# Token sums in half passes, four tiles first in the last round, and a shorter end for the last tile

## The chip, the cores and the metric

The kernel runs on one core of a Trainium2 chip. The metric is the device time of one execution in microseconds (us), lower being better; the time before is the median of 3 runs. TensorE (PE) does the matmuls, and its weight loads are counted apart (PEld). VectorE (DVE), ScalarE (ACT) and GpSimd (POOL) do elementwise work, and SyncE (SP) issues DMAs. The engines run side by side, each through its own list of instructions in order, and wait for each other on semaphores.

## The reference

One layer of a hybrid attention and state-space network over 128 context and 512 latent tokens, 640 in all, with 1024 channels, in float32. The change touches its last part, the MLP and the last layer norm:

```python
h  = layer_norm(x) * (1 + sc2) + sh2
ff = jnp.square(jax.nn.relu(h @ p['w_mlp1'] + p['b_mlp1'])) @ p['w_mlp2'] + p['b_mlp2']
x  = layer_norm(ALPHA * x + g2 * ff, p['ln2_g'], p['ln2_b'])
```

## The kernel before

Each float32 operand of a matmul is kept as two parts, an upper and a lower one, and each product takes three matmuls. ScalarE writes the upper part of a weight block (split_hi, tile whi), VectorE subtracts it from the block to get the lower one (split_lo, wlo, L2280), and TensorE waits for that on the semaphore lo_done.

The 4096 hidden channels come in four rounds of 1024. In each, a first product makes hidden channels for all 640 tokens, and a second one adds them into five tiles of 128 tokens (tile 0 is the context, 1 to 4 are latent), each in two halves of 512 channels (c = 0, 1).

- Round 0 makes its hidden channels in 8 units of 48 matmuls (the first four in two halves of 24). For each, VectorE adds the bias and takes the maximum with 0 (L2927), which also frees the unit's PSUM banks, squares (L2929) and subtracts the upper part (L2932); ScalarE makes that upper part between them. TensorE begins unit n when VectorE's L2927 of unit n - 2 is done. The second product goes over (c, b), where b is a half of the 1024 hidden channels: 12 matmuls for each tile, so 60 for each (c, b), and VectorE adds each finished bank into xo (L2987).
- Rounds 1 to 3 use Strassen's scheme for the first product: 7 products in place of 8 for each 2 by 2 block. It needs four sums of the token operand, each with an upper and a lower part. They are made once, in round 0, by operand_sum on VectorE (L2956, ten sums, and L2965, four lower parts) and upper_sum on ScalarE (L2211). Before the change eight sums and two lower parts stand between round 0's units, two sums and two lower parts behind them, ahead of the second product's first addition. TensorE needs them at the start of round 1. GpSimd makes the sums of the weights for each block (L934 to L940) and two lower parts (L943).
- The last round's second product (last_products) has its own order, the table LAST. For c = 0 it does three tiles with b = 0, then the same three with b = 1; for that it needs the second lower part (L2280). Then come single units of 24 matmuls, whose c = 1 weights are split into the tiles hh and hl (w3h, w3l; last_lo, L3064, two of them, after the first and the second unit on VectorE). For each unit VectorE runs last_unit: add the bank to xo (L3055), multiply by the gate row g2r (L3057), add ALPHA times x1 (L3058), and statistics (L3060). When a tile is whole it gathers the statistics (L2307), adds EPS (L3085), and ScalarE takes the root. One unit later, in finish, it inverts the root (L3068) and makes two weighing passes over 1024 channels (L2321: less the mean, times ln2_g; L2322: times the inverse, plus ln2_b), and SyncE stores the tile (L792). The last tile's second half comes in two units of 256 channels.

The gate rows g2r and x1 of tiles 0 to 2 are loaded in the last round (L780, L778), when the memory that they take is no longer needed by Strassen's scheme. The whole order is written out by hand.

## Time and profile before

| What | us |
|---|---|
| median of 3 runs | 1574.17 (1572.31 to 1575.41) |
| the profiled execution | 1572.93 |
| its span, first to last instruction | 1571.2 |
| TensorE busy | 1505.6 (96%) |
| VectorE busy | 1015.6 (65%) |
| ScalarE busy | 688.3 (44%) |
| GpSimd busy | 208.0 (13%) |

An engine's busy time is the sum over its instructions, and the share is of the span. Matmuls overlap in a pipeline, so TensorE at 96% says that it seldom stands idle. Times in the rows below count from the span's start. Round 0's first product runs from about 1128 to 1186, the last round's second product from 1501 to the end.

### The profile page before, as it was taken

To read this page: it belongs to the slowest core of one execution; us is meant where nothing else is said; L and a number is where in the kernel's file an instruction comes from. 1 tells how busy PE (TensorE), PEld (TensorE's weight loads), DVE (VectorE), ACT (ScalarE), POOL (GpSimd) and SP (SyncE) were. 2 spreads that over 40 slices of the span, in tenths; PEclk is the share of its full clock that TensorE was granted. 3 is DMA by queue.
4 is the path that set the end of the run, shared out by engine and by line. 5 is a ranking of instruction groups with operands and counts; after the bars stand their busy time and mean duration, and the time that the engine had idled before them with its cause. 6 is when DMAs were issued, how large, how long until landed. Compare 5 with 4: busy or idle time off the path is not lost.

```text
span 1571.2 us, 25180 instructions
## 1 busy us (share of the span) xinstructions
PE 1505.6 (96%) x10114; PEld 1397.2 (89%) x10114; DVE 1015.6 (65%) x1410; ACT 688.3 (44%) x1258; POOL 208.0 (13%) x227
## 2 busy tenths in 40 slices
PE   4999999999999989999999999999989999999997
PEld 2899999999999989898766899999988898998976
DVE  5666566658555688988876443438876462653768
ACT  2443333343563266777676342323523262451630
POOL 1011122100101100000000001000001441611700
PEclk9999999999999999999999999999999999999999
DMA  9555555543777767877620346235212132131251
GB/s 318 177 177 193 176 185 178 179 137 118 227 231 260 246 232 243 266 225 220 226 105 27 126 154 201 95 107 189 94 54 81 54 108 81 54 108 54 81 174 67
DMA packets 152511, 244.62 MB, mean 156 GB/s; under 512 B 8112, under 2 KB 110240, under 8 KB 149344
## 3 DMA queue, kind: packets, MB, share of 16 engines
q1 hardware_dynamic: 129232, 174.59, 33.4%
q0 software_dynamic: 12304, 47.72, 8.3%
q10 hardware_dynamic: 10880, 20.97, 5.2%
q8 instruction: 68, 1.11, 0.3%
q14 instruction: 27, 0.22, 0.0%
HBM read 196.63 MB, written 46.63 MB: 155 GB/s over the span
## 4 chain that ended last, share of the span: by engine, by line
PE 78%; DVE 12%; ACT 6%; issue 1%; DMA 1%; SPq 1%; ACTq 0%; DVEq 0%
PE acc L957 57%; PE tp L957 18%; DVE wlo L2280 2%; ACT arena L1914 2%; PE tp L1424 1%; ACT whi L1692 1%; DVE arena L2554 1%; PE tp L1085 1%; DMA arena<-in_w_mod 1%; DVE arena L2385 1%; DMA arena<-decay_sums_t 1%; DVE arena L2555 1%; ACT whi L2072 1%; DVE wlo L2755 1%; DVE arena L2956 1%
## 5 line engine op out<-in xcount | busy, mean ns | idle before, releaser
L957 PE MATMUL acc<-hh,whi 128*128 128x322 f32 (+1 forms) x1068 | 288.2, 319 | 8.0 <-DVE cst L2927 3.6
L957 PE MATMUL acc<-hl,whi 128*128 128x322 f32 (+1 forms) x1068 | 281.7, 313 | 0.0
L957 PE MATMUL acc<-hh,wlo 128*128 128x322 f32 (+1 forms) x1068 | 281.0, 312 | 0.0
L957 PEld LDWEIGHTS acc<-hh,whi 128*128 128x128 f32 x1068 | 189.2, 191 | 12.7 <-issue 10.4
L957 PEld LDWEIGHTS acc<-hl,whi 128*128 128x128 f32 x1068 | 190.7, 191 | 0.0
L957 PEld LDWEIGHTS acc<-hh,wlo 128*128 128x128 f32 x1068 | 190.4, 191 | 0.0
L957 PE MATMUL acc<-whi,hh 128*128 128x256 f32 x640 | 183.1, 286 | 0.0
L957 PE MATMUL acc<-whi,hl 128*128 128x256 f32 x640 | 179.7, 281 | 0.0
L957 PE MATMUL acc<-wlo,hh 128*128 128x256 f32 x640 | 179.7, 281 | 0.0
L2280 DVE TENSOR_TENSOR wlo<-raw,whi 128x2048 fp32r<-128x2048 f32 x62 | 143.5, 2315 | 34.9 <-ACT whi L1692 34.9
L1692 ACT ACTIVATE whi<-raw 128x2048 fp32r<-128x2048 f32 x62 | 118.2, 1907 | 76.9 <-PE tp L957 53.9
L957 PE MATMUL tp<-arena 128*32 128x256 f32 (+4 forms) x774 | 135.0, 373 | 10.0 <-DVE arena L2573 3.7
L2385 DVE SCALAR_TENSOR_TENSOR arena<-arena,colp 128x642 f32<-128x642 f32 x128 | 113.6, 888 | 16.9 <-DVE arena L2383 1.2
L957 PEld LDWEIGHTS acc<-whi,hh 128*128 128x128 f32 x640 | 120.6, 188 | 0.6 <-issue 0.2
L957 PEld LDWEIGHTS acc<-wlo,hh 128*128 128x128 f32 x640 | 120.5, 188 | 0.2
L957 PEld LDWEIGHTS acc<-whi,hl 128*128 128x128 f32 x640 | 120.5, 188 | 0.0
L957 PEld LDWEIGHTS tp<-arena 128*128 128x128 f32 (+1 forms) x774 | 85.0, 164 | 35.0 <-issue 19.3
L1914 ACT ACTIVATE arena<-arena,time_steps 128x128 f32<-128x128 f32 x320 | 97.7, 391 | 25.6 <-PE acc L957 18.0
L1704 ACT ACTIVATE arena<-acc 128x644 f32<-128x644 f32 (+2 forms) x94 | 47.8, 508 | 126.2 <-PE acc L957 126.1
L1762 ACT ACTIVATE arena<-arena 128x642 f32<-128x642 f32 x32 | 23.8, 743 | 112.4 <-DVE arena L2385 112.4
L957 PE MATMUL acc<-whi,fh 128*128 128x512 f32 x176 | 69.7, 396 | 1.6 <-DVE wlo L2280 1.6
L957 PE MATMUL acc<-wlo,fh 128*128 128x512 f32 x176 | 69.6, 395 | 0.0
(361 smaller groups left out, 3127.5 us busy)
## 6 DMA issues: line engine op xcount, KB each, us to landing
raw<-in_w_in SPq DMA_DIRECT2D x38, 1024.0 KB, 8.6
raw<-in_w_mlp SPq DMA_DIRECT2D x32, 1024.0 KB, 5.3
arena<-in_w_mod SPq DMA_DIRECT2D x24, 1024.0 KB, 8.2
arena<-decay_sums_t ACTq DMA_DIRECT2D x40, 512.0 KB, 6.0
arena<-xs_nat SPq DMA_DIRECT2D x8, 1024.0 KB, 10.7
raw<-in_w_ssd_o SPq DMA_DIRECT2D x8, 1024.0 KB, 6.6
y_nat<-arena POOLq DMA_DIRECT2D x6, 1024.0 KB, 7.6
arena<-y_nat SPq DMA_DIRECT2D x6, 1024.0 KB, 6.0
```

Of the source, the lines that this page charges most:

```text
L957: return pe.matmul(out, l, r, start=first, stop=last)
L1085: last = pe.transpose(dst, cvs[:, n % 2, tok(t):tok(t) + P], ident)
L1424: last = pe.transpose(tp[:, j // 4, (j % 4) * P:(j % 4 + 1) * P], pr[:, u, j * P:(j + 1) * P], ident)
L1692: act.activation(whi[:, slot], raw[:, slot], ACT.Copy).then_inc(hi["sem"], step(hi))
L1704: act.activation(dst, src, func).then_inc(free["sem"], step(free))
L1762: act.activation(cvs[:, n % 2], cvo[:, n % 2], ACT.Silu).then_inc(silu["sem"], step(silu))
L1914: last = act.activation(ee[:, b, d, r], abc[:, b, d, r], ACT.Relu, bias=dta[:, c, h:h + 1], scale=-1.0)
L2072: last = act.activation(whi[:, slot, k], raw[:, slot, k], ACT.Copy, scale=colp[:, n:n + 1])
L2280: dve.tensor_tensor(wlo[:, slot], raw[:, slot], whi[:, slot].bitcast(F32), ALU.subtract).then_inc(lo["sem"], step(lo))
L2385: ins = dve.scalar_tensor_tensor(o, x[:, t:t + NCONV], w(t), o, ALU.mult, ALU.add)
L2554: do(dve.tensor_tensor(ee[:, b], ee[:, b], cbm[:, :, g].unsqueeze(2).broadcast_to([P, 2, R, P]), ALU.mult))
L2555: dve.tensor_tensor(ee[:, b, 0], ee[:, b, 0], ee[:, b, 1], ALU.add).then_inc(m_ok["sem"], step(m_ok))
```

## The change

1. Round 0: no operand sum and no lower part stands between the units any more. Eight sums stand now ahead of the second product's first addition on VectorE, the other two and the four lower parts between its halves c = 0 and c = 1. The upper parts on ScalarE move with them.
2. Last round: four tiles, not three, are done with b = 0 and then b = 1, ahead of the units with c = 1. The lower parts of the c = 1 weights (last_lo) stay behind the first and the second unit.
3. The first weighing pass (begun) stands right behind the statistics, ahead of the wait for the root; finish keeps the inverse and the second pass.
4. For the last tile, GpSimd multiplies xo by the gate row and adds ALPHA times x1 beforehand, with three new instructions of 1024 channels. VectorE's unit for that tile has then two elementwise instructions in place of three: the bank times the gate row, and the sum.
5. The last tile's second weighing pass and its store come in two halves of 512 channels.

```diff

-    LAST = [(t, c, 0, 2 * BW) for t, c in ((0, 0), (1, 0), (2, 0), (0, 1), (1, 1), (2, 1), (3, 0), (3, 1), (4, 0))]
+    LAST = [(t, c, 0, 2 * BW) for t, c in ((0, 0), (1, 0), (2, 0), (3, 0), (0, 1), (1, 1), (2, 1), (3, 1), (4, 0))]
     LAST += [(4, 1, 0, BW), (4, 1, BW, BW)]
...
         sp.dma_start(lnr2[:, 1], a["ln2_b"][0].partition_broadcast(P)).then_inc(s["rows2_in"], 16)
-        for t in range(NT):
+        for t in range(NT - 1):
             sp.wait_ge(s["final_ok"], t + 1)
             dst = y_p[0] if t == 0 else y_s[0, (t - 1) * P:t * P]
             sp.dma_start(dst, xo[:, t]).then_inc(s["out_done"], 16)
-        sp.wait_ge(s["out_done"], 16 * NT)
+        for b in range(2):
+            sp.wait_ge(s["final_ok"], NT + b)
+            cols = slice(b * 2 * BW, (b + 1) * 2 * BW)
+            sp.dma_start(y_s[0, (NT - 2) * P:, cols], xo[:, NT - 1, cols]).then_inc(s["out_done"], 16)
+        sp.wait_ge(s["out_done"], 16 * (NT + 1))

...
                 step(raws[b], 2)
+
+        t = NT - 1
+        po.wait_ge(s["rows2_in"], 16 * 4)
+        po.wait_ge(s["acc_free"], U_MLP + KT + 3 * 2 * NT)
+        po.tensor_tensor(xo[:, t], xo[:, t], g2r[:, 1], ALU.mult).then_inc(sums["sem"], step(sums))
+        po.tensor_scalar(x1[:, t], x1[:, t], ALPHA, None, ALU.mult).then_inc(sums["sem"], step(sums))
+        po.wait_ge(sums["sem"], value(sums))
+        po.tensor_tensor(xo[:, t], xo[:, t], x1[:, t], ALU.add).then_inc(sums["sem"], step(sums))

...
                 pe.wait_ge(lo["sem"], due(lo))
-                for i in range(3):
+                for i in range(NT - 1):
                     if b == 0:
                         step(free)
                         bank_free(i, False)
                     last = ff_products(last_bank(i), i, *whole[0][b], b, waits=i == 0)
                     if b:
                         last.then_inc(ready["sem"], step(ready))
-            for i in range(3, len(LAST)):
+            for i in range(NT - 1, len(LAST)):
                 t, c, at, n = LAST[i]
...
                 for b in range(2):
-                    if i == 3:
+                    if i == NT - 1:
                         pe.wait_ge(lo["sem"], due(lo))
...
                 step(ready)
-                if n in (3, 4):
-                    upper_sum(n - 3)
                 if n % 2 == 1:
...
             if r == 0:
-                upper_sum(2)
-                upper_sum(3)
+                for n in range(3):
+                    upper_sum(n)
             act.wait_ge(half["sem"], due(half))
             split_hi(0)
             step(ready, NT)
             act.wait_ge(ready["sem"], value(ready))
             split_hi(1)
+            if r == 0:
+                upper_sum(3)
             act.wait_ge(half["sem"], due(half))
...
                     split_lo(n // 2 % 2)
-                if 1 <= n <= 4:
-                    operand_sum(2 * n - 2)
-                    operand_sum(2 * n - 1)
-                elif n in (5, 6):
-                    operand_sum(10 + n - 5)

...
             if r == 0:
-                for n in (8, 9, 12, 13):
+                for n in range(8):
                     operand_sum(n)
...
                     split_lo(1)
+                    if r == 0:
+                        for n in range(8, 14):
+                            operand_sum(n)
                 else:
...
             dve.wait_ge(ready["sem"], due(ready))
-            dve.tensor_tensor(xo[:, t, cols], xo[:, t, cols], last_bank(i)[:, 0:n], ALU.add).then_inc(free["sem"], step(free))
-            dve.wait_ge(free["sem"], value(free))
-            do(dve.tensor_tensor(xo[:, t, cols], xo[:, t, cols], g2r[:, min(t, 1), cols], ALU.mult))
-            do(dve.scalar_tensor_tensor(xo[:, t, cols], x1[:, t, cols], ALPHA, xo[:, t, cols], ALU.mult, ALU.add))
+            if t < NT - 1:
+                dve.tensor_tensor(xo[:, t, cols], xo[:, t, cols], last_bank(i)[:, 0:n], ALU.add).then_inc(free["sem"], step(free))
+                dve.wait_ge(free["sem"], value(free))
+                do(dve.tensor_tensor(xo[:, t, cols], xo[:, t, cols], g2r[:, min(t, 1), cols], ALU.mult))
+                do(dve.scalar_tensor_tensor(xo[:, t, cols], x1[:, t, cols], ALPHA, xo[:, t, cols], ALU.mult, ALU.add))
+            else:
+                if c == 0:
+                    dve.wait_ge(s["sum_ok"], LANDED + 4 * 3 * S_BLOCKS + 3)
+                dve.tensor_tensor(x1[:, t, cols], last_bank(i)[:, 0:n], g2r[:, 1, cols], ALU.mult).then_inc(free["sem"], step(free))
+                dve.wait_ge(free["sem"], value(free))
+                do(dve.tensor_tensor(xo[:, t, cols], xo[:, t, cols], x1[:, t, cols], ALU.add))
             for b in range(at // BW, (at + n) // BW):
...

+        def begun(t):
+
+            if t == 0:
+                dve.wait_ge(s["rows2_in"], 16 * 6)
+            do(dve.scalar_tensor_tensor(xo[:, t], xo[:, t], mv[:, t, 0:1], lnr2[:, 0], ALU.subtract, ALU.mult))
+
         def finish(t):
             dve.wait_ge(dev["sem"], due(dev))
             do(dve.reciprocal(mv[:, t, 2:3], mv[:, t, 2:3]))
-            weighed(t, xo[:, t], lnr2).then_inc(s["final_ok"], 1)
+            for b in range(2 if t == NT - 1 else 1):
+                cols = slice(b * 2 * BW, (b + 1) * 2 * BW) if t == NT - 1 else slice(0, D)
+                dve.scalar_tensor_tensor(xo[:, t, cols], xo[:, t, cols], mv[:, t, 2:3], lnr2[:, 1, cols],
+                                         ALU.mult, ALU.add).then_inc(s["final_ok"], 1)

...
             if whole is not None:
-                if whole == 0:
-                    dve.wait_ge(s["rows2_in"], 16 * 6)
                 finish(whole)
                 whole = None
+            if i in (0, 1):
+                last_lo(i)
             if i in WHOLE:
                 whole = WHOLE[i]
                 dve.wait_ge(dv["sem"], value(dv))
                 gathered(whole)
                 dve.tensor_scalar(mv[:, whole, 2:3], mv[:, whole, 1:2], EPS, None, ALU.add).then_inc(var["sem"], step(var))
-            if i in (0, 1):
-                last_lo(i)
+                begun(whole)
         finish(whole)
```

What VectorE finds in round 0 behind the first block's split_lo (hl and hh are the operand's parts, cst the unit's channels), before:

```order
L2280 TENSOR_TENSOR wlo<-raw,whi 128x2048 [waits hi_done]
L2956 TENSOR_TENSOR arena<-hh 128x1280 [waits x_in3_then_x1_out]
L2956 TENSOR_TENSOR arena<-hl 128x1280 [waits dve_step]
L2927 TENSOR_SCALAR cst<-tp,colp 128x640 [waits acc_ready,dve_step]
L2929 TENSOR_TENSOR time_steps<-cst 128x640 [waits acc_free]
L2932 TENSOR_TENSOR fl<-time_steps,fh 128x640 [waits square_ok,relu_ok]
L2956 TENSOR_TENSOR arena<-arena 128x1280
L2956 TENSOR_TENSOR arena<-hh 128x1280 [waits mod_in7_then_t_sum]
```

and after:

```order
L2292 TENSOR_TENSOR wlo<-raw,whi 128x2048 [waits hi_done]
L2939 TENSOR_SCALAR cst<-tp,colp 128x640 [waits acc_ready]
L2941 TENSOR_TENSOR time_steps<-cst 128x640 [waits acc_free]
L2944 TENSOR_TENSOR fl<-time_steps,fh 128x640 [waits square_ok,relu_ok]
L2939 TENSOR_SCALAR cst<-tp,colp 128x640 [waits acc_ready]
```

The two sums between the split and the next unit's L2927 (L2939 now) are gone, and so are those behind that unit.

VectorE at the end of round 0's first product, from the last split_lo on, before:

```order
L2280 TENSOR_TENSOR wlo<-raw,whi 128x2048 [waits hi_done]
L2956 TENSOR_TENSOR hl_full<-hh,arena 128x4x320
L2956 TENSOR_TENSOR hl_full<-hl_full,hl 128x4x320 [waits dve_step]
L2965 TENSOR_TENSOR t_lo<-arena,t_hi 128x1280 [waits x_in_then_t_hi,mod_in7_then_t_sum]
L2965 TENSOR_TENSOR hl<-hl_full,hh 128x4x320 [waits x_in_then_t_hi]
L2987 TENSOR_TENSOR arena<-arena,acc 128x512 [waits acc_ready]
L2280 TENSOR_TENSOR wlo<-raw,whi 128x2048 [waits hi_done]
```

and after:

```order
L2292 TENSOR_TENSOR wlo<-raw,whi 128x2048 [waits hi_done]
L2963 TENSOR_TENSOR arena<-hh 128x1280 [waits x_in3_then_x1_out]
L2963 TENSOR_TENSOR arena<-hl 128x1280 [waits dve_step]
L2963 TENSOR_TENSOR arena<-arena 128x1280 [waits dve_step]
L2963 TENSOR_TENSOR arena<-hh 128x1280 [waits mod_in7_then_t_sum]
L2963 TENSOR_TENSOR arena<-hl 128x1280 [waits dve_step]
L2963 TENSOR_TENSOR arena<-arena 128x1280 [waits dve_step]
L2963 TENSOR_TENSOR arena<-hh,arena 128x1280 [waits mod_in7_then_t_sum]
L2963 TENSOR_TENSOR arena<-arena,hl 128x1280 [waits dve_step]
L2994 TENSOR_TENSOR arena<-arena,acc 128x512 [waits acc_ready,mod_in7_then_t_sum]
L2292 TENSOR_TENSOR wlo<-raw,whi 128x2048 [waits hi_done]
```

Eight sums, each waiting for the one before it, now stand ahead of the first addition of a bank and of the next split_lo.

GpSimd at the end of its list, after (before, the list ended with the second of these rows):

```order
L947 TENSOR_TENSOR wlo<-time_steps,whi 128x512 [waits mod_in1_then_entry_hi]
L947 TENSOR_TENSOR wlo<-time_steps,whi 128x512 [waits mod_in1_then_entry_hi,mod_in6_then_pool_lo]
L956 TENSOR_TENSOR arena<-arena 128x1024 [waits acc_free,rows2_in,mod_in6_then_pool_lo]
L957 TENSOR_SCALAR arena<-arena 128x1024
L959 TENSOR_TENSOR arena<-arena 128x1024 [waits mod_in0_then_sum_ok]
```

The three last rows are new. The first of them waits for the gate rows (rows2_in), and the second follows it without a wait.

VectorE's end, from the last tile's two units of 256 channels on, before:

```order
L3055 TENSOR_TENSOR arena<-arena,acc 128x256 [waits acc_ready]
L3057 TENSOR_TENSOR arena<-arena 128x256 [waits acc_free]
L3058 SCALAR_TENSOR_TENSOR arena<-arena 128x256 [waits dve_step]
L3060 BN_STATS st<-arena 128x6 [waits dve_step]
L3055 TENSOR_TENSOR arena<-arena,acc 128x256 [waits acc_ready]
L3057 TENSOR_TENSOR arena<-arena 128x256 [waits acc_free]
L3058 SCALAR_TENSOR_TENSOR arena<-arena 128x256 [waits dve_step]
L3060 BN_STATS st<-arena 128x6 [waits dve_step]
L2307 BN_AGGR mv<-st 128x2 [waits dve_step]
L3085 TENSOR_SCALAR mv<-mv 128x1 [waits dve_step]
L3068 RECIPROCAL mv<-mv 128x1 [waits dev_ok]
L2321 SCALAR_TENSOR_TENSOR arena<-arena,mv,raw 128x1024 [waits dve_step]
L2322 SCALAR_TENSOR_TENSOR arena<-arena,mv,raw 128x1024 [waits dve_step]
```

and after:

```order
L3073 TENSOR_TENSOR arena<-acc,arena 128x256 [waits acc_ready]
L3075 TENSOR_TENSOR arena<-arena 128x256 [waits acc_free]
L3077 BN_STATS st<-arena 128x6 [waits dve_step]
L3073 TENSOR_TENSOR arena<-acc,arena 128x256 [waits acc_ready]
L3075 TENSOR_TENSOR arena<-arena 128x256 [waits acc_free]
L3077 BN_STATS st<-arena 128x6 [waits dve_step]
L2319 BN_AGGR mv<-st 128x2 [waits dve_step]
L3111 TENSOR_SCALAR mv<-mv 128x1 [waits dve_step]
L3087 SCALAR_TENSOR_TENSOR arena<-arena,mv,raw 128x1024
L3091 RECIPROCAL mv<-mv 128x1 [waits dev_ok,dve_step]
L3094 SCALAR_TENSOR_TENSOR arena<-arena,mv,raw 128x512 [waits dve_step]
L3094 SCALAR_TENSOR_TENSOR arena<-arena,mv,raw 128x512
```

Each unit has one instruction less, the first weighing pass stands ahead of the inverse, and the second one is in halves.

## Rows read from the trace of the kernel before

**Rows 1.** TensorE's timeline: start, us, engine, line, operation, tiles, form, [idle, releaser].

```profile
1154.12 0.67 PE L957 MATMUL acc<-hh,whi 128*128 128x320 f32 x2 [3.65 <-DVE cst L2927]
...
1171.29 0.53 PE L957 MATMUL tp<-hh,whi 128*128 128x320 f32 x2 [1.35 <-DVE cst L2927]
```

**Rows 2.** VectorE's timeline around the first of these waits.

```profile
1143.48 0.88 DVE L2927 TENSOR_SCALAR cst<-acc,colp 128x640 f32<-128x640 f32 x1
...
1146.10 0.82 DVE L2932 TENSOR_TENSOR fl<-time_steps,fh 128x640 fp32r<-128x640 f32 x1 [0.88 <-ACT fh L2197]
1147.83 2.29 DVE L2280 TENSOR_TENSOR wlo<-raw,whi 128x2048 fp32r<-128x2048 f32 x1 [0.91 <-ACT whi L1692]
1150.04 1.48 DVE L2956 TENSOR_TENSOR arena<-hh 128x1280 f32<-128x1280 f32 x1
...
1153.09 0.89 DVE L2927 TENSOR_SCALAR cst<-tp,colp 128x640 f32<-128x640 f32 x1
```

**Rows 3.** Stretches: length; PE, PEld, DVE, ACT, POOL busy; PEclk, DMA share, GB/s.

```profile
1114.88:1117.48 2.60, 0.01 (x1) 0.04 (x1) 2.40 (x2) 2.05 (x3) 0.00 (x0) 0.87 0.00 0
1117.48:1120.00 2.52, 2.52 (x9) 2.52 (x10) 2.45 (x6) 1.24 (x1) 0.00 (x0) 0.50 0.42 110
...
1156.00:1158.00 2.00, 2.00 (x10) 2.00 (x9) 1.97 (x3) 0.00 (x0) 0.00 (x0) 0.56 0.01 4
...
1524.55:1528.00 3.45, 3.45 (x15) 2.82 (x16) 3.02 (x6) 0.00 (x0) 0.00 (x0) 1.00 0.00 0
```

**Rows 4.** The chain of waits in order of time: start us, us, engine, tile, line, instructions.

```profile
1171.29 14.29 PE tp L957 x96
...
1196.75 2.80 PE tp L957 x12
```

**Rows 5.** TensorE's timeline, 1508 to 1572, the rows with idle time.

```profile
1511.16 0.50 PE L957 MATMUL acc<-whi,fh 128*128 128x512 f32 x1 [1.64 <-DVE wlo L2280]
...
1524.55 0.51 PE L957 MATMUL acc<-hh,fh 128*128 128x512 f32 x1 [1.91 <-DVE hl L3064]
```

**Rows 6.** VectorE's timeline, 1500 to 1572.

```profile
1507.00 0.82 DVE L3015 TENSOR_TENSOR fl<-cst,fh 128x640 fp32r<-128x640 f32 x1 [2.27 <-ACT cst L2182]
1508.81 2.29 DVE L2280 TENSOR_TENSOR wlo<-raw,whi 128x2048 fp32r<-128x2048 f32 x1 [0.98 <-ACT whi L1692]
1514.34 0.69 DVE L3055 TENSOR_TENSOR arena<-arena,acc 128x512 f32<-128x512 f32 x1 [3.24 <-PE acc L957]
...
1515.79 0.69 DVE L3058 SCALAR_TENSOR_TENSOR arena<-arena 128x512 f32<-128x512 f32 x1
...
1561.98 0.42 DVE L3058 SCALAR_TENSOR_TENSOR arena<-arena 128x256 f32<-128x256 f32 x1
...
1566.84 1.28 DVE L2322 SCALAR_TENSOR_TENSOR arena<-arena,mv,raw 128x1024 f32<-128x1024 f32 x1
```

**Rows 7.** Waits from 1500 to 1572: engine, line, for whom: us, times, longest us.

```profile
DVE arena L3055 <- PE acc L957: 5.1, 3, 3.2
...
DVE arena L3055 <- PE tp L957: 2.2, 1, 2.2
...
DVE mv L3068 <- ACT mv L1699: 0.3, 1, 0.3
```

**Rows 8.** VectorE's timeline in the second round, 1254 to 1258.

```profile
1254.83 1.18 DVE L3015 TENSOR_TENSOR fl<-cst,fh 128x640 fp32r<-128x640 f32 x1 [0.96 <-ACT cst L2182]
...
1256.40 1.33 DVE L2973 TENSOR_TENSOR wlo<-raw,whi 128x512 fp32r<-128x512 f32 x1
```

**Rows 9.** GpSimd's timeline, 1254 to 1258.

```profile
1254.04 1.29 POOL L934 TENSOR_TENSOR time_steps<-raw 128x512 f32<-128x512 f32 x1 [0.72 <-DVE wlo L2973]
1255.41 1.76 POOL L936 TENSOR_TENSOR raw<-raw 128x512 f32<-128x512 f32 x1
```

**Rows 10.** Line 780, the loads of the gate rows: issue to landing.

```profile
DMA to landing us min/median/max: 9.6/10.3/11.1
```

**Rows 11.** Line 792, the stores of the results: issue to landing.

```profile
DMA to landing us min/median/max: 2.6/2.6/2.6
```

## The prediction

> **What bounds the kernel now.** I read the page first. TensorE is busy for 96% of the span and VectorE for 65%: the time is set by TensorE's matmuls, and VectorE counts where TensorE waits for it and behind TensorE's last matmul. So I took TensorE's timeline in the two stretches that the change touches, then VectorE's beside it, then the waits. All times count in the frame of before; what a stretch gains comes off everything behind it.
>
> In round 0 TensorE stands for 3.65 us ahead of unit 4 and for 1.35 us ahead of unit 6, both times for VectorE's L2927 [rows 1]. VectorE's rows show why: the split that unit 4 needs ends at 1150.1, then come two operand sums of 1.5 each, and only at 1153.09 the L2927 of unit 2, which frees what unit 4 waits for [rows 2]. The wait has a price behind it: TensorE's granted clock is 0.56 on average from 1156 to 1158, so the half level (1.2 GHz) for most of it [rows 3].
>
> In the last round TensorE waits twice: 1.64 us for the lower part of the b = 1 weights (L2280), and 1.91 us for last_lo [rows 5]. But VectorE is the nearer limit there. From the first addition at 1514.34 to its end at 1568.12 (1566.84 + 1.28) are 53.78 us [rows 6]. In them it waits 1.9 (5.1 less the 3.24 ahead of the first) and 2.2 for banks and 0.3 for the last root, 4.3 with rounding [rows 6, 7]. So 49.5 us of the stretch are VectorE's own chain.
>
> **Round 0, sums moved away.** Behind the split, L2927 of unit 2 can start at 1150.04 in place of 1153.09 [rows 2]. TensorE went on at 1154.12, 1.03 after that instruction's start [rows 1, 2]; now it goes on at 1151.07, idle 0.6 after 1150.47. Gain 3.05. Units 4 and 5 took from 1154.12 to 1169.94 (1171.29 less 1.35 [rows 1]), 15.8, where the two units 6 and 7 took 14.29 at full clock [rows 4]. I take it that no fall of the clock follows an idle time of 0.6: behind the 1.91 us in the last round it stayed at 1.00, behind 2.60 us at 1114.88 it was 0.50 [rows 3, 5]. Gain 1.5. The 1.35 ahead of unit 6 goes as well, because VectorE has for each pair of units of 14.1 us only two times 3.4 (1143.48 to 1146.92 [rows 2]), a wait of 0.9 and a split of 2.2, some 10 us. With overlaps counted (a matmul's end and the next one's start differ by 0.16) round 0's second product begins 6.1 us earlier, at T = 1179.3.
>
> What is late next? The sums now meet the second product. VectorE's last split of round 0's first product ends at T + 6.7: L2927 to L2932 of unit 7 3.4, ScalarE's upper part in 1.9 of which 1.1 shows, split 2.2. Eight sums of 1.51 (start to start [rows 2]) end at T + 18.8, where before the first bank came at T + 16.8 (14 + 2.8 for a tile [rows 4]): its addition is 2 us late. Behind it stands the split for c = 1, b = 0; ScalarE's upper part for it now waits behind upper_sum(2), which needs sum 8, and so it ends at T + 22.0 and the split at T + 24.3. TensorE asks for it at T + 28: 3.7 us of cover. The other six, 9 us, stand behind the last split of that product at T + 32.3 and end by T + 42, or T + 46 where GpSimd's sums of the weights come between; round 1's first Strassen product asks for them at T + 56. I cost this at nothing. SyncE's load of the next weights waits for the split at T + 24.3 and so is issued 4.7 later than before relative to T; its data are wanted by ScalarE at T + 42, so that is covered too.
>
> **Last round, four tiles first.** The fourth tile with b = 0 gives TensorE 2.8 us of work where it stood 1.64 [rows 4, 5]. Taken alone this removes that wait and, since VectorE gets both last_lo done in time, the 1.91 too; but VectorE's chain starts at the first tile's b = 1. Before, that began at 1511.16 and VectorE's addition 3.18 later at 1514.34 [rows 5, 6]. Now b = 1 begins at 1512.15 at the earliest (1511.16 - 1.64 + 2.80, less the overlap of 0.16), 1.0 later.
>
> **GpSimd's three instructions, a new cost ahead of that point.** Their start is set by the gate rows: issued at 1495.0, landed 11.1 later [rows 10], so 1506.1. No row shows a GpSimd instruction of 1024 elements; those of 512 take 1.29 undisturbed [rows 9], so I take 2.6 (for tensor_scalar between 1.3 and 2.6, chosen 2.6). What they do to VectorE is in the rows: at 1254.83 L3015, with two inputs in SBUF, starts inside GpSimd's L934, which ends at 1255.33, and takes 1.18 instead of 0.82 [rows 6, 8, 9]; L936 then takes 1.76 instead of 1.29, and the split behind it, started at 1256.40, takes 1.33 instead of some 0.7 (instructions of 512 elements take 0.69 [rows 6]), its end 0.56 after L936's [rows 8, 9]. So one of the two stands until the other is through, and they take turns. Here: the first instruction runs from 1506.2 to 1508.8; L3015, due at 1507.00, stands until then and ends at 1509.5; the second one gets its turn from 1509.4 to 1512.0; the split L2280, due at 1509.5, stands until 1512.0 and ends at 1514.2 in place of 1511.1 [rows 6]. TensorE's b = 1 begins at 1514.25, 3.1 later than before, and VectorE's chain at 1517.4. The bounds of this term: 1.0 later (no turn lost) and 5.7 (the second GpSimd instruction, which has no wait of its own, takes its turn ahead of L3015, and the third one ahead of the split).
>
> On the instruction's length the Trainium skill has a price of its own: "GPSIMD Engine Reference", section "Elementwise — side-by-side cycle accounting", gives 4497 ns for a tensor_tensor of 2048 float32, so an estimate of 2.25 us for 1024, where the rows of 512 give 2.6. By the page the chain would start some 0.3 to 0.7 us earlier. The rows decide.
>
> **VectorE's chain and the end.** The last tile loses L3058 three times: once with 512 channels, 0.73 from start to start, twice with 256, 0.46 each [rows 6]: 1.65. The wait for the root (0.3 [rows 7]) goes, since the first weighing pass of 1.3 stands in it, and it was not counted in the 49.5. The second pass in halves costs 0.1 more. Does VectorE still wait for banks? TensorE supplies a c = 1 tile in 5.6, VectorE needs 2.84 for the unit, 0.4 for statistics, 2.7 for both passes, 5.9: it falls behind at once and stays behind, since two units and two splits of 2.2 have already put it 2 us back. So the chain is 49.5 - 1.65 + 0.1 = 48.0 without waits, from 1517.4 to 1565.4. Before it ended at 1568.12: 2.7 earlier. Behind it stands the store: 2.6 from issue to landing for 512 KB [rows 11]. The first half is on its way 0.7 before the second; for the second, half the bytes, I take 0.3 less (between 0, all of it fixed, and 1.3, all of it bytes). Together 3.0.
>
> The Trainium skill, "DMA: Bandwidth & Descriptors", section "Anatomy of one DMA — SWDGE (gpsimd) path", has a fixed 2.0 us and then bytes by 436 GB/s: an estimate of 0.6 less for 256 KB. No run here shows a store of that size at the end; by it the sum would be 0.3 larger.
>
> **Sum.** 6.1 + 3.0 = 9.1. From the profiled execution, 1572.93 (its span 1571.2 and 1.7 around it), this gives 1563.8. That execution lies 1.2 below the median of the runs; against the median, 1574.17 - 9.1 = 1565.0 us, which is what I forecast.
>
> **Rivals.**
> - GpSimd costs VectorE nothing that TensorE sees (its second instruction is short, or VectorE slips in ahead of it). For it: many VectorE instructions in the Strassen rounds lie beside GpSimd's without loss, those that read a bank. Against: L3015 and the split read only SBUF, as in [rows 8]. Then the chain starts at 1515.3, 2.1 earlier: 1563.0.
> - GpSimd keeps its turn over two instructions, because nothing waits between them. Then the split ends at 1516.8, 2.6 later, TensorE has stood 4.5 us, more than the 2.60 behind which the clock fell [rows 3], and loses some 1.7 more at half clock: 1569.3. Against it: in the rows each one waiting got the next turn; but there GpSimd had a semaphore between.
> - The gain in round 0 is smaller: another wait stands where L2927's was (the weights' lower part ends at 1150.1, only 0.4 before TensorE is ready), or the clock falls all the same. That takes 1.5 to 6.1 off: 1566.5 to 1571.1.
> - Slower than before: the eight sums at the head of the second product. If each took more than some 2.0 longer than its 1.5, the split for c = 1, b = 0 would come 16 us late, 12.3 beyond its cover of 3.7, and TensorE would stand that long: over 1577.3 in place of 1565.0. It decides from 3.5 us for a sum. Against it: GpSimd, the only one seen to lengthen such instructions, has nothing to do until the next weights land at about T + 30.
>
> **Chances.** The forecast's case 0.50 (1563.5 to 1566.5), GpSimd free of cost 0.20, GpSimd's double turn 0.10, smaller gain in round 0 0.15, slower 0.05. The range of 1561.8 to 1569.3 holds the first two with the bounds of the store (0 to 1.3) and most of the third and the fourth. A measurement of this kernel can tell about 0.2%, 3.1 us, from no change. All of the first three cases and most of the fourth are faster by more: 0.93. Within it 0.03, slower 0.04.
>
> **What the profile after would show.** Right: TensorE idle ahead of unit 4 for 0.6, nothing ahead of unit 6, granted clock 1.00 from 1151 to 1179; the eight sums from about 1186 to 1198 and no wait of TensorE in the second product; GpSimd's three instructions from about 1500 (1506 less 6.1), L3015 and the split beside them lengthened to some 2.5 and 4.7, a wait of TensorE of 2 us behind four tiles; then VectorE without waits for banks up to its end. Wrong: a split of 2.3 there (first rival), a half clock behind it (second), any TensorE wait between the sums and round 1 (fourth). The forecast fails most easily in the order in which GpSimd and VectorE take turns in those 8 us.

## The result and the profile after

| | before | after |
|---|---|---|
| median of 4 runs each, same chip | 1573.47 (1572.31 to 1575.41) | 1561.68 (1560.47 to 1561.81) |
| ratio, with its 95% interval | | 0.9922 [0.9905, 0.9939] |
| the profiled execution | 1572.93 | 1561.81 |
| its span | 1571.16 | 1560.02 |

The kernel became 11.8 us faster, where 9.1 were forecast. The time lies 0.1 below the forecast's range. The page of after has nearly the same balance as before: busy time by engine, and the chain that ended last by engine. It doesn't say where the time went; only the stretches do.

```profile
PE 1502.3 (96%) x10114; PEld 1393.8 (89%) x10114; DVE 1020.9 (65%) x1408; ACT 688.6 (44%) x1258; POOL 222.0 (14%) x230
...
PE 77%; DVE 13%; ACT 5%; DMA 2%; issue 1%; SPq 1%; ACTq 0%; DVEq 0%
```

**Round 0.** TensorE's timeline of after has one row with idle time from 1119 to 1240, where before had two [rows 1]:

```profile
1150.82 0.53 PE L969 MATMUL acc<-hh,whi 128*128 128x320 f32 x2 [0.62 <-DVE cst L2939]
```

VectorE's rows say why: L2939 (L2927 before) stands now directly behind the split, where two sums stood [rows 2], and the eight sums fill the head of the second product:

```profile
1147.58 2.29 DVE L2292 TENSOR_TENSOR wlo<-raw,whi 128x2048 fp32r<-128x2048 f32 x1 [0.91 <-ACT whi L1704]
1149.79 0.88 DVE L2939 TENSOR_SCALAR cst<-tp,colp 128x640 f32<-128x640 f32 x1
...
1185.76 1.48 DVE L2963 TENSOR_TENSOR arena<-hh 128x1280 f32<-128x1280 f32 x1
...
1196.44 1.49 DVE L2963 TENSOR_TENSOR arena<-arena,hl 128x1280 f32<-128x1280 f32 x1
1197.96 0.69 DVE L2994 TENSOR_TENSOR arena<-arena,acc 128x512 f32<-128x512 f32 x1
1201.07 2.29 DVE L2292 TENSOR_TENSOR wlo<-raw,whi 128x2048 fp32r<-128x2048 f32 x1 [2.42 <-ACT whi L1704]
```

The next table is by stretch: length, busy time of PE, PEld, DVE, ACT and POOL, granted clock, DMA share, GB/s. The second row is the one that answers to the half clock of before from 1156 [rows 3]: the clock holds. The first shows the half clock that both kernels have behind an earlier idle time of 2.6 us, at round 0's start.

```profile
1118.46:1122.00 3.54, 3.54 (x14) 3.54 (x15) 3.40 (x9) 1.36 (x2) 0.00 (x0) 0.55 0.67 181
1150.82:1157.00 6.18, 6.18 (x42) 6.18 (x43) 3.98 (x5) 2.82 (x3) 0.00 (x0) 1.00 0.49 174
```

**The last round.** TensorE's two waits of 1.64 and 1.91 [rows 5] are gone (0.19 is left, at 1520). Its first matmul with b = 1 follows the last one with b = 0 after 0.39, where the others follow each other after 0.23, and it starts 0.05 behind the end of VectorE's split (1505.83, below). So the four tiles cover that split almost to its end, with nothing to spare:

```profile
1505.49 0.40 PE L969 MATMUL acc<-whi,fl 128*128 128x512 f32 x1
1505.88 0.50 PE L969 MATMUL acc<-whi,fh 128*128 128x512 f32 x1
```

VectorE's timeline, from the last operand to the first tile's chain, and then its end, to be held against [rows 6]:

```profile
1500.58 0.82 DVE L3025 TENSOR_TENSOR fl<-cst,fh 128x640 fp32r<-128x640 f32 x1 [2.26 <-ACT cst L2194]
1502.39 3.44 DVE L2292 TENSOR_TENSOR wlo<-raw,whi 128x2048 fp32r<-128x2048 f32 x1 [0.98 <-ACT whi L1704]
1509.08 0.69 DVE L3066 TENSOR_TENSOR arena<-arena,acc 128x512 f32<-128x512 f32 x1 [3.25 <-PE acc L969]
1509.80 1.69 DVE L3068 TENSOR_TENSOR arena<-arena 128x512 f32<-128x512 f32 x1
...
1555.94 0.16 DVE L3091 RECIPROCAL mv<-mv 128x1 f32<-128x1 f32 x1
1556.14 1.41 DVE L3094 SCALAR_TENSOR_TENSOR arena<-arena,mv,raw 128x512 f32<-128x512 f32 x2
```

GpSimd's three new instructions beside it:

```profile
1500.61 3.07 POOL L956 TENSOR_TENSOR arena<-arena 128x1024 f32<-128x1024 f32 x1 [20.08 <-issue]
1503.66 4.81 POOL L957 TENSOR_SCALAR arena<-arena 128x1024 f32<-128x1024 f32 x1
1508.55 2.39 POOL L959 TENSOR_TENSOR arena<-arena 128x1024 f32<-128x1024 f32 x1
```

And the stores of the two halves, where before one of 512 KB took 2.6 [rows 11]:

```profile
DMA to landing us min/median/max: 2.0/2.1/2.1
```

The 11.15 us of the span by stretch, each boundary read in both timelines:

| stretch | before | after | gain | forecast |
|---|---|---|---|---|
| start to TensorE's stop ahead of unit 4 | 1150.47 | 1150.20 | 0.27 | 0 |
| from there to round 0's second product | 34.95 | 28.79 | 6.16 | 6.1 |
| from there to the last round's second product | 315.54 | 315.54 | 0 | 0 |
| from there to VectorE's first addition | 13.38 | 14.55 | -1.17 | -3.1 |
| from there to VectorE's end | 53.78 | 48.47 | 5.31 | 5.8 |
| from there to the span's end | 3.04 | 2.47 | 0.57 | 0.3 |

So the large term was right to 0.1, and the one that failed is the fourth: TensorE waited 0.2 at most for the split behind the four tiles, where 2.1 were forecast. What is left between 11.15 and 11.8 is that before's profiled execution lay 0.5 below its median, and after's 0.1 above.

### The profile page after: what moved, and what is told of

The parts are those of the page before. It is cut to its first block, busy times and chain, and to the rows that moved or that the text cites. A ratio compares the mean times of both kernels' runs of the same rounds, so it can differ in the third digit from the quotient of the medians.

```text
span 1560.0 us, 25183 instructions
## 1 busy us (share of the span) xinstructions
PE 1502.3 (96%) x10114; PEld 1393.8 (89%) x10114; DVE 1020.9 (65%) x1408; ACT 688.6 (44%) x1258; POOL 222.0 (14%) x230
## 4 chain that ended last, share of the span: by engine, by line
PE 77%; DVE 13%; ACT 5%; DMA 2%; issue 1%; SPq 1%; ACTq 0%; DVEq 0%
PE acc L969 57%; PE tp L969 17%; ACT arena L1926 2%; DMA arena<-decay_sums_t 1%; PE tp L1436 1%; DVE wlo L2292 1%; DVE arena L2566 1%; PE tp L1097 1%; DMA arena<-in_w_mod 1%; DVE arena L2397 1%; DVE arena L2567 1%; ACT whi L2084 1%; DVE wlo L2767 1%; PE tp L1483 1%; DVE arena L2600 1%
## 5 line engine op out<-in xcount | busy, mean ns | idle before, releaser
L969 PE MATMUL tp<-arena 128*32 128x256 f32 (+4 forms) x774 | 135.2, 373 | 10.9 <-DVE arena L2585 3.8
L969 PE MATMUL acc<-whi,fh 128*128 128x512 f32 x184 | 72.9, 396 | 0.0
```

Source lines behind the costliest of these rows:

```text
L969: return pe.matmul(out, l, r, start=first, stop=last)
```

## The experiments

Two places were in dispute: which part of round 0's gain is wait and which is clock, and what GpSimd's instructions do to VectorE. Every run has a profile, and the stretches of the table above are read in each; the median is given where there were five runs (four for end_only), beside the ratio to before. Medians move by about 1 us with the chip and the execution, stretches hardly at all: with the sums moved as in after, the one from TensorE's stop to T takes 28.77 to 28.79 in every profile, and the one from T to the last round 315.54 or 315.55 in all but all_head's. So single profiles are compared by their stretches. T is the begin of round 0's second product.

**Does the gain fall into two parts that add up?** sums_only has the move of the sums and nothing else, end_only everything but that.

```diff
 # sums_only: the last round, GpSimd's part, the passes and the store as before
-        LAST = [... (0, 0), (1, 0), (2, 0), (3, 0), (0, 1), (1, 1), (2, 1), (3, 1), (4, 0) ...]
+        LAST = [... (0, 0), (1, 0), (2, 0), (0, 1), (1, 1), (2, 1), (3, 0), (3, 1), (4, 0) ...]
 # end_only: the sums as before
+                    if 1 <= n <= 4:
+                        operand_sum(2 * n - 2)
+                        operand_sum(2 * n - 1)
```

> Before, with only the token sums moved (eight at the head of round 0's second product, the rest between its halves); the last round is as before. Theory A (each part's gain is its own): 6.2 us off the profiled span of 1571.2, so about 1565.0, TensorE idle 0.6 ahead of unit 4 and not at all ahead of unit 6, no half clock from 1150 on. Rival B (part of this gain is given back later, for instance the last round starts earlier but its loads do not): under 5 us off.

> After, with the token sums put back where they were before; all changes of the last round stay. Theory A: 5.0 us off the span of before (11.2 less 6.2), about 1566.2, with the waits of 3.65 and 1.35 us and the half clock back. Rival B (the parts need each other): over 6 or under 4 us off.

Measured: sums_only 1567.0, ratio 0.9963 [0.9949, 0.9977]; end_only 1566.5, ratio 0.9958 [0.9942, 0.9975]. Against before in the same runs (1572.6) that is 5.6 and 6.1, together 11.7 of 11.8: the parts add up. By stretches they are 6.18 (34.95 to 28.77) and 5.67 (70.20 to 64.53). In sums_only the stretch to T takes 28.77, as in after, and the last round is before's to 0.01 (70.21 from its begin to the end, 70.20 there), waits of 1.65 and 1.91 included. In end_only the stretch to T takes 34.96, as in before, its wait is 3.67, and the last round takes 64.53. That is 1.0 less than in after's profile, since VectorE and GpSimd took turns in another order there (see "What does GpSimd cost VectorE?"). These two also settle that the eight sums under the second product cost nothing.

**How much is wait, and how much clock?** one_sum puts one of the sums back behind the first split, two_sums two.

```diff
 # one_sum (two_sums has operand_sum(1) too)
+                    if n == 1:
+                        operand_sum(0)
...
-                for n in range(8):
+                for n in range(1, 8):
```

> After, with only the first sum put back behind unit 1's split. TensorE is to stand 2.1 us ahead of unit 4. Theory A (an idle time near the 1.91 behind which the clock stayed does not make it fall): second product 1.5 later than in after. Rival C (it falls as behind the 2.60 at 1114.88): 3.2 later.

> After, with the first two of the eight sums put back behind unit 1's split, as before; six stay at the head of the second product. Theory A (the wait of 3.65 is these two sums, and the fall of the clock hangs on it): TensorE idle 3.6 to 3.7 ahead of unit 4, then some 3.4 us at half clock, round 0's second product 4.6 to 4.8 us later than in after. Rival C (the half clock came from somewhere else): only 3.05 later.

Measured: one_sum waits 2.14 where after waits 0.62, and behind it the clock falls. Its stretches (columns as above):

```profile
1149.00:1152.40 3.40, 1.26 (x9) 1.03 (x8) 3.33 (x4) 0.00 (x0) 0.00 (x0) 1.00 0.53 143
1152.40:1155.80 3.40, 3.40 (x15) 3.40 (x14) 2.44 (x3) 0.75 (x2) 0.00 (x0) 0.50 0.43 165
1155.80:1160.00 4.20, 4.20 (x30) 4.20 (x30) 2.46 (x2) 2.53 (x2) 0.00 (x0) 1.00 0.02 6
```

15 matmuls in 3.4 us at half clock, 30 in 4.2 at full: the stretch to T is 31.85, 3.06 longer than after's. Half of that (1.52) is the sum, the other half the clock. So the theory in which the clock falls already behind some 2 us was right here, and the forecast's two points (1.91 without a fall, 2.60 with one) had left that open. two_sums waits 3.65, stands at half clock for 6.8 us from 1153.1, and its stretch is 34.41, 5.6 longer: 3.03 of wait and 2.6 of clock, where I expected 4.6 to 4.8 in all.

In before itself the clock's share is not a cause of its own. end_only has before's order of sums, and its clock was at the half level for longer:

```profile
1152.10:1158.90 6.80, 5.38 (x20) 5.41 (x21) 5.79 (x7) 0.74 (x1) 0.00 (x0) 0.50 0.30 117
```

In before it was there for 3.4 us (0.51 from 1154.30 to 1157.70). Yet the stretch to T is the same, 34.96 to 34.95: TensorE's second wait, ahead of unit 6, is 0.46 in end_only and 1.35 in before. In both, the L2927 that ends it starts 19.8 behind TensorE's stop. So with sums between the units VectorE's list sets T, and what the clock costs comes off the next wait. The clock's price is seen only where no second wait takes it up, as in one_sum and two_sums.

**What are the sums' dividing and the four tiles worth?** all_head puts all fourteen ahead of the second product's first addition. three_tiles undoes the four tiles alone.

```diff
 # all_head (ScalarE's last upper_sum moves ahead too)
-                for n in range(8):
+                for n in range(14):
...
-                        if r == 0:
-                            for n in range(8, 14):
-                                operand_sum(n)
 # three_tiles: LAST and the two loop bounds as before
```

> After, with all ten sums and four lower parts at the head of round 0's second product, none between its halves. Theory A (the cover of the head is 3.6 us; unit 9 to 14 take 9 us more): the split for c = 1, b = 0 ends 9 us later, TensorE stands some 5.4 us ahead of c = 1 and the clock falls behind it, 7 us in all: span about 1567. Rival D (there is more cover than I reckon, dividing the sums in two is worth nothing): TensorE does not stand, span 1560.

> After, with three tiles first in the last round as before; GpSimd's three instructions, the early first pass and the halves stay. Theory A: VectorE's first addition stays at 1509.1, because it hangs on the split that GpSimd delays, but TensorE stands 2.9 us ahead of b = 1 and again for both last_lo, its last matmul comes some 5.4 later, and VectorE waits for banks again: span 3.9 later, about 1563.9. Rival E (VectorE's chain alone sets the end): within 0.5 of 1560.0.

Measured: in all_head the stretch from T to the last round takes 318.29 in place of 315.54. TensorE waits 2.49 for the split of c = 1, b = 0, less than expected, and the clock stays at full. The cover for that split was larger than I said, since VectorE itself waits 2.42 for ScalarE's upper part there in after (the row at 1201.07 above), and with six more sums ahead that wait is used up first. The dividing is worth 2.75. In three_tiles the last round takes 70.03, 4.5 more than after's and 5.5 more than after_again's (64.52, below), which has the same order of turns. TensorE's two waits are back and one of them is longer, 2.73, with 3.4 us of half clock behind it:

```profile
1505.37 0.50 PE L969 MATMUL acc<-whi,fh 128*128 128x512 f32 x1 [2.73 <-DVE wlo L2292]
...
1520.33 0.50 PE L969 MATMUL acc<-hh,fh 128*128 128x512 f32 x1 [1.92 <-DVE hl L3081]
```

Both rows are TensorE's, with the idle time ahead. In sums_only, with three tiles too but without GpSimd's instructions, the first was 1.65: the 1.08 more is the later end of the split, which TensorE sees with three tiles. VectorE's first addition did not stay where it was, as I had expected, but came 1.5 later (16.03 behind the round's begin, 14.55 in after). So GpSimd's work needs the fourth tile as its cover.

**The passes and the store.** late_pass puts the first weighing pass back behind the root, whole_store the last tile's second pass and store back into one.

```diff
 # late_pass
             def finish(t):
...
+                begun(t)
...
-                    begun(whole)
 # whole_store
-                for b in range(2 if t == NT - 1 else 1):
-                    cols = slice(b * 2 * BW, (b + 1) * 2 * BW) if t == NT - 1 else slice(0, D)
+                for b in range(1):
+                    cols = slice(0, D)
```

> After, with the first weighing pass behind the inverse again (as before). Theory A: only the wait for the last root comes back, 0.3 us: span 1560.3. Rival F (the early pass also fills gaps at the other tiles): over 1 us later.

> After, with the last tile's second pass and store whole. Theory A: VectorE's end 0.1 earlier, landing 2.6 after its issue in place of 2.0 for a half: span 0.5 later, 1560.5. Rival G (the store's time is all fixed): 0.1 earlier.

Measured: by their spans both came out shorter than after, 1559.0 and 1559.2 to 1560.0. That is not their edit. In both, GpSimd and VectorE take turns in another order than in after's profile (next part), and beside a run with that order, after_again, VectorE's chain is 0.75 longer in late_pass (48.23 to 47.48). The early pass is worth that, where I had counted 0.3 for the root: it also filled a bank wait of 0.28. For the 0.2 that are left no row has a wait. VectorE's rows of late_pass with a wait:

```profile
1527.73 0.69 DVE L3066 TENSOR_TENSOR arena<-arena,tp 128x512 f32<-128x512 f32 x1 [0.28 <-PE tp L969]
...
1553.62 0.16 DVE L3091 RECIPROCAL mv<-mv 128x1 f32<-128x1 f32 x1 [0.27 <-ACT mv L1711]
```

In whole_store the chain is 0.13 shorter and the stretch behind it 3.04 in place of 2.47: the halves are worth 0.44. The landings are 2.6 for 512 KB and 2.0 to 2.1 for 256 KB. The estimate of 0.6 that I had worked out from the Trainium skill's bytes by 436 GB/s ("DMA: Bandwidth & Descriptors", "Anatomy of one DMA — SWDGE (gpsimd) path") was nearer to that difference than my 0.3. Its fixed part of about 2.0 does not fit these stores, which SyncE issues and not GpSimd: 2.0 and 0.6 would be 2.6 for 256 KB.

**What does GpSimd cost VectorE?** This is the step that failed. after_again is the changed kernel once more; no_gpsimd gives the last tile's two elementwise steps back to VectorE; both_early loads the gate rows ahead of x1 and puts the tensor_scalar first, which needs no gate row; rows_first moves the loads alone.

```diff
 # both_early (rows_first has the first two lines only)
-                    sp.dma_start(x1[:, 0:3], ...)     # ahead of the gate rows' load
+                    sp.dma_start(x1[:, 0:3], ...)     # behind it
...
+            po.tensor_scalar(x1[:, t], x1[:, t], ALPHA, ...)   # ahead of the wait for the gate rows
-            po.tensor_scalar(x1[:, t], x1[:, t], ALPHA, ...)
 # no_gpsimd
-            po.tensor_tensor(xo[:, t], ...)
-            po.tensor_scalar(x1[:, t], ...)
-            po.tensor_tensor(xo[:, t], ...)
...
-                if t < NT - 1:
+                if t < NT:
```

> The changed kernel once more, beside the next two. Theory H (GpSimd and VectorE take turns, and which order they take hangs on when the gate rows land): either VectorE's second fl is first (split 3.4, later L3068 at 1.7 instead of 0.7, chain from first addition to VectorE's end 48.5) or GpSimd is (fl 2.1 to 2.6, split 3.1, chain 47.5); runs 1560.4 to 1561.9.

> After, with the last tile done by VectorE alone as the others, no GpSimd instructions. The recorded sum (GpSimd makes b = 1 2.1 later and takes 1.65 off the chain): 0.45 faster than after. Theory H (GpSimd costs 0 to 1.15 of the end, the rest hidden by the fourth tile): chain 49.1, first addition at most 0.2 earlier, 0.5 to 1.5 slower than after.

> After, with GpSimd's tensor_scalar ahead of its wait for the gate rows (it needs only x1) and the gate rows loaded ahead of x1. Theory H: GpSimd's two other instructions are through before or beside the fl parts, the split is late by under 1, nothing stands on L3068, chain 47.5: 0 to 1.0 us faster than after. Rival I (what GpSimd delays is not on the path): no difference in any stage.

> After, with the gate rows loaded ahead of x1, GpSimd's three instructions in their order. Theory H: the first starts 2 to 4 us earlier against VectorE's work, the third is through before the first addition, L3068 takes 0.7, chain 47.5. The split is lengthened by up to 2.4 if the third instruction has its turn there, and TensorE then stands up to 1.2. Rival I: chain 48.5 as in after.

Measured, each beside its stretch from the last round's begin to the end:

| | median, us | ratio | split, us | first L3068, us | stretch, us |
|---|---|---|---|---|---|
| after | 1561.68 | 0.9922 [0.9905, 0.9939] | 3.44 | 1.69 | 65.49 |
| after_again | 1560.73 | 0.9922 [0.9909, 0.9936] | 3.12 | 0.69 | 64.52 |
| no_gpsimd | 1560.87 | 0.9926 [0.9913, 0.9940] | 2.29 | 0.69 | 65.83 |
| both_early | 1559.89 | 0.9914 [0.9901, 0.9928] | 2.29 | 0.69 | 64.31 |
| rows_first (1 run) | 1562.27 | | 3.43 | 0.69 | 65.94 |

The term of my sum that failed shows in two of these runs. Without GpSimd's instructions (no_gpsimd) the first addition comes 14.27 behind the round's begin, 0.9 later than before's 13.38: that is the fourth tile. With them it comes at 14.55 (after) and 14.59 (after_again), and VectorE's chain behind it is 49.1 without them, as theory H had it, and 48.47 or 47.48 with them. So what GpSimd does delays it by 0.3, where my sum has 2.1. The split ends 1.2 later with them, and the fourth tile hides 1.0 of that: in no_gpsimd the split is done at 1503.41, but TensorE's b = 1 begins only at 1504.46, behind the four tiles.

The same kernel has two orders of turns. In after's profile VectorE's L3025 starts 0.03 ahead of GpSimd's first instruction, and GpSimd's third one meets the first L3068 on VectorE's chain, which stands 1.0 for it. In after_again GpSimd starts first, and all three are through ahead of the first addition. What differs ahead of it is the landing of the gate rows: the second of their two loads landed 11.9 after its issue in after and 11.0 in after_again. In the three traces with VectorE first (after, all_head, two_inputs) it was 11.9 to 12.3, in the nine with GpSimd first and the loads in this order 10.9 to 11.3. GpSimd's timeline of after_again:

```profile
1499.52 2.41 POOL L956 TENSOR_TENSOR arena<-arena 128x1024 f32<-128x1024 f32 x1 [19.20 <-issue]
1501.91 3.34 POOL L957 TENSOR_SCALAR arena<-arena 128x1024 f32<-128x1024 f32 x1
1505.34 2.57 POOL L959 TENSOR_TENSOR arena<-arena 128x1024 f32<-128x1024 f32 x1
```

VectorE's timeline beside it:

```profile
1500.36 2.25 DVE L3025 TENSOR_TENSOR fl<-cst,fh 128x640 fp32r<-128x640 f32 x1 [2.26 <-ACT cst L2194]
1502.54 3.12 DVE L2292 TENSOR_TENSOR wlo<-raw,whi 128x2048 fp32r<-128x2048 f32 x1
1508.91 0.69 DVE L3066 TENSOR_TENSOR arena<-arena,acc 128x512 f32<-128x512 f32 x1 [3.25 <-PE acc L969]
1509.63 0.69 DVE L3068 TENSOR_TENSOR arena<-arena 128x512 f32<-128x512 f32 x1
```

Handing the work to GpSimd is worth 0.3 in the one order (65.83 to 65.49) and 1.3 in the other. The medians of after_again and no_gpsimd are the same within their spread, so this gain of part 4 of the change is seen in the stretches alone. no_gpsimd's stretch also speaks against my recorded sum, by which it should have been 0.45 shorter than after's and not 0.34 longer. both_early has neither loss, and its stretch is the shortest, by 0.2; its median of 1559.89, the lowest of all, isn't told apart from after's. rows_first shows that the earlier load alone is worse: GpSimd's third instruction then meets the split, and TensorE does wait behind its four tiles, for 1.49:

```profile
1502.18 3.10 POOL L959 TENSOR_TENSOR arena<-arena 128x1024 f32<-128x1024 f32 x1
1503.99 3.43 DVE L2292 TENSOR_TENSOR wlo<-raw,whi 128x2048 fp32r<-128x2048 f32 x1 [0.98 <-ACT whi L1704]
1507.48 0.50 PE L969 MATMUL acc<-whi,fh 128*128 128x512 f32 x1 [1.49 <-DVE wlo L2292]
```

The three rows are of three engines, GpSimd, VectorE and TensorE. L959 is a tensor_tensor and ends at 1505.28; the split ends 2.14 behind that.

**Why did the split wait so little?** In after_again the split starts at 1502.54 inside GpSimd's L957, which goes on to 1505.25, and yet takes only 3.12: without company it takes 2.29. By my forecast it should have stood to 1505.25 and ended at 1507.5. L957 is a tensor_scalar, with one input in SBUF. So in two_inputs it is replaced by a tensor_tensor of the same size with two (x1 + x1, which leaves out ALPHA for the last tile and puts 2 in its place).

```diff
-            po.tensor_scalar(x1[:, t], x1[:, t], ALPHA, None, ALU.mult)...
+            po.tensor_tensor(x1[:, t], x1[:, t], x1[:, t], ALU.add)...
```

> After, with GpSimd's tensor_scalar of x1 replaced by a tensor_tensor that adds x1 to itself (the factor ALPHA of the last tile is left out for 2). Theory J (the forecast failed because it counted a one-input instruction like a two-input one): where GpSimd's first instruction is ahead of VectorE's second fl, the split stands until this second one is through, 4.6 to 4.9 in place of 3.1, and TensorE stands 1.1 to 1.6 behind its four tiles. Rival K (GpSimd's second instruction always lets VectorE in halfway): split 3.1 as before, TensorE does not stand. If fl is ahead of GpSimd's first, both expect a split of 3.4 and L3068 longer than 0.7.

> The kernel end_only with GpSimd's tensor_scalar of x1 replaced by a tensor_tensor that adds x1 to itself (the factor ALPHA of the last tile is left out for 2). The run two_inputs had VectorE's fl ahead of GpSimd's first instruction and so did not decide; end_only's own trace had GpSimd ahead. Theory J: with GpSimd ahead, the split stands to the end of the second instruction, so over 3.6 in place of 3.1. Rival K: 3.1 or less. With fl ahead: 3.4 for both, undecided.

> The kernel late_pass with the same replacement (the factor ALPHA of the last tile is left out for 2). The same question and the same expectations: theory J a split over 3.6 where GpSimd's first instruction is ahead of the second fl, rival K 3.1 or less, and 3.4 where fl is ahead.

two_inputs itself fell into the other order and decided nothing (span 1558.6). The edit on top of end_only and on top of late_pass did. GpSimd's timeline in end_only:

```profile
1507.95 3.35 POOL L957 TENSOR_SCALAR arena<-arena 128x1024 f32<-128x1024 f32 x1
1511.38 2.57 POOL L959 TENSOR_TENSOR arena<-arena 128x1024 f32<-128x1024 f32 x1
```

VectorE's split beside it, in end_only:

```profile
1508.58 3.12 DVE L2292 TENSOR_TENSOR wlo<-raw,whi 128x2048 fp32r<-128x2048 f32 x1
```

GpSimd's timeline in two_inputs_end_only:

```profile
1507.73 2.48 POOL L957 TENSOR_TENSOR arena<-arena 128x1024 f32<-128x1024 f32 x1
1510.28 4.32 POOL L959 TENSOR_TENSOR arena<-arena 128x1024 f32<-128x1024 f32 x1
```

VectorE's split beside it:

```profile
1508.38 3.98 DVE L2292 TENSOR_TENSOR wlo<-raw,whi 128x2048 fp32r<-128x2048 f32 x1
```

And TensorE, which now waits for it:

```profile
1512.41 0.50 PE L969 MATMUL acc<-whi,fh 128*128 128x512 f32 x1 [0.86 <-DVE wlo L2292]
```

With two inputs the split stands until GpSimd's L957 ends (1510.21, 1.83 after the split's start) and needs 2.15 more; TensorE waits 0.86 for it. In two_inputs_late_pass it is 3.98 and 0.92. That decides for theory J, with less than the 4.6 to 4.9 and the 1.1 to 1.6 that I had expected for the first of the three. With one input, in end_only, it loses 0.83 and ends at 1511.70; had it stood until L957's end at 1511.30, it would have ended at 1513.45. So a rule of turns that holds between two-input instructions [rows 8, 9] does not hold where GpSimd's is a tensor_scalar with one. The Trainium skill ("SBUF — State Buffer", "Who interferes with whom") says that a VectorE instruction with two inputs in SBUF contends with a GpSimd instruction that reads SBUF, over a shared pair of ports that is an exclusive lock. For tensor_tensor against tensor_tensor the rows agree; beside a tensor_scalar the split loses a part of the time only, and the measurement decides. The runs change the operation together with its number of inputs, so which of the two counts is not shown, nor what lets VectorE in. L957 itself loses next to nothing by it: it takes 3.35 in end_only, and 3.29 in both_early, where only short instructions of VectorE lie beside it.

## Why the prediction came out as it did

- **Wait and clock in round 0, and the 1.35 ahead of unit 6: right** (6.16 for 6.1). TensorE goes on behind 0.62 for a forecast of 0.6, the clock stays up, and with one_sum and two_sums the wait and the clock's share come back. My step from "behind the 1.91 it stayed, behind 2.60 it was 0.50" to an idle time of 0.6 held; as a rule for what lies between, all_head (2.49, no fall) and one_sum (2.14, a fall) refute it. The sum of 3.05, 1.5 and 1.35 came out because all three are gone in after. As causes they are one: the sums in VectorE's list set T in before, and without the fall of its clock TensorE would have waited that much longer ahead of unit 6 (end_only against before).
- **The eight sums cost nothing: right.** They run from 1185.8 to 1197.9 (forecast 1186 to 1198), and the rival on the slower side never came near. The stated cover of 3.7 was too small, since it left out that VectorE waits itself.
- **The fourth tile's 1.0: right** (0.9 by no_gpsimd).
- **The step that failed** is "the second one gets its turn from 1509.4 to 1512.0; the split L2280, due at 1509.5, stands until 1512.0 and ends at 1514.2", which made 2.1 of the 3.1 us for the later first addition. Measured are 0.3 of 1.2. The order was another one in after: the split stood for GpSimd's first instruction and was 1.15 longer, and L957 came behind it. In after_again it started 0.4 later, amid L957, and was 0.83 longer. In both it ended 1.2 later than in no_gpsimd, and the fourth tile covers 1.0 of that.
- **How the error of 1.9 divides.** With the instruction that I had priced (two_inputs_end_only) the first addition comes 15.42 behind the round's begin, so 2.0 later than before and not 3.1; in end_only it comes at 14.58. So 0.84 is that a tensor_scalar was taken for a tensor_tensor. The other 1.1 lies in the times of two tensor_tensor instructions. They take 2.42 and 2.48, not 2.6 each. And the second starts when the first ends, 1.5 behind L3015's start, where I had it wait for VectorE's turn until 2.4.
- **The first rival**, "GpSimd costs VectorE nothing that TensorE sees", 1563.0, with a chance of 0.20, is nearly what happened. Its reason was right in part only. VectorE did slip in, but the split still ended 1.2 later, and GpSimd's third instruction cost the chain 1.0 in after's profile. That the cover would be just enough I had not foreseen: in rows_first the split ends 1.5 later still, and TensorE waits 1.49.
- **VectorE's chain, 48.0: right** for the order without that stand (47.48), 0.5 short of after's 48.47. The early pass was worth 0.75, where 0.3 was taken.
- **The store's 0.3: too small**, it is 0.44 with the extra instruction counted, 0.57 without.
- **The range.** Its low end rested on the first rival with the bounds of the store. What the profiled execution lay below its median (1.2) I had carried over to the result; of after's four runs the profiled one was the longest. With the failed step that makes 3.3 between 1565.0 and 1561.68: 2.0 from the stretches, 1.3 from this.

What stays open: why VectorE gets in amid a tensor_scalar of GpSimd. The 0.27 ahead of TensorE's stop I put down to chance: unit 0 began 1.0 later in after, and the half clock behind it lasted 3.4 us in place of 6.8, which gave 1.26 back. The other profiles bear this out. From unit 0's first matmul to the stop TensorE takes 33.0 in before, 31.7 in after, and 30.8 in late_pass, no_gpsimd and three_tiles, where the clock did not fall there; nothing in this stretch differs between these kernels.

## What to carry to other kernels

Read a stretch's gain from what waits last in it: moving 15 us of sums and lower parts on VectorE (ten instructions of 1.5) to where TensorE had slack gave 6.2. Of that 4.4 were seen as waits (3.03 and 1.35) and the rest as clock, but a longer half clock left the stretch as it was (end_only). So what waits last is to be counted, and not each loss on the way to it. Work handed to GpSimd beside a chain of two-input VectorE instructions needs cover for the turns that it takes (here a fourth tile of 2.8 us), and where 0.9 us of a load's landing goes with another order of turns, two profiles of one kernel can differ by 1 us, so that small edits are compared only at equal order. Turns between engines are to be priced by kind of instruction (0.84 us here), not by size alone.

## What the runs showed of the hardware

- GpSimd on 128x1024 float32, its times being rough in a profile: tensor_tensor 2.40 to 2.42 (after_again, both_early), tensor_scalar 3.29 (both_early) to 3.35 (end_only). The operation with fewer inputs is the slower.
- A two-input VectorE instruction that takes 2.29 alone took 3.12 when it started amid a GpSimd tensor_scalar (end_only, after_again). Amid a GpSimd tensor_tensor it stood until that ended and took 2.15 from there (after, rows_first, two_inputs_end_only). Where it had stood and was at work when the tensor_scalar started, it lost nothing more, and the tensor_scalar took 4.81 (after).
- TensorE's granted clock fell to the half level behind idle times of 2.14 (one_sum) and 2.73 (three_tiles), but stayed up behind 2.49 (all_head) and 1.91. The same 2.6 us ahead of round 0 led to half clock in before, after and most of the others and to none in late_pass, no_gpsimd, three_tiles and two_inputs_late_pass. The half level lasted 3.4 us or 6.8. Idle times of one length went both ways, and what decides is not shown.
